# Sample readouts packed on TensorE's row and column groups, and head norms with tokens on partitions, in a hybrid decoder step

## The chip, the core and the metric

The kernel runs on one core of a Trainium2 chip. The metric is the device time of one execution in microseconds (us), and less is better. TensorE is called PE in the profile, its weight loads PEld, VectorE DVE, ScalarE ACT, GpSimd POOL and SyncE SP.

## The reference, cut to what matters

The program is one inference step of a two-layer trunk with model width 1024, for a prompt of 512 tokens and for 8 samples of one token each (520 columns, N). Layer 0 begins with a mixer of four GLA heads (key width 64, value width 128) and four retention heads (128 and 128); each head has a recurrent state matrix:

```python
    z = x @ w_in                      # q_g, k_g, v_g, a_lr, r_g, q_r, k_r, v_r, g_r
    # per head: S_t = diag(a_t) S_{t-1} + k_t^T v_t,  o_t = q_t S_t, in chunks over the prompt
    o_g, s_gla = chunked_gated_linear_attention(...)
    o_g = rms_head_norm(o_g, g_gla) * jax.nn.silu(heads(r_g, GLA_HEADS))
    o_r, s_ret = chunked_gated_linear_attention(...)
    o_r = group_norm_heads(o_r, g_ret, b_ret) * jax.nn.silu(heads(g_r, RET_HEADS))
    y = jnp.concatenate([o_g, o_r], axis=-1) @ w_out
```

The prompt starts from a zero state. Each of the 8 samples has a state of its own for each head: it is decayed, the outer product of the sample's key and value is added, it is stored, and it is read with the sample's query. The head norms are over the 128 values of one head at one token. What follows (layer norm, a gated ConvFFN, a short-convolution mixer, another ConvFFN) is not changed.

## The kernel before

Activations stand with features on partitions and the 520 tokens along the free axis. A weight unit is 1024 rows by 256 columns; SP loads it into one of three buffers, ACT makes its rounded part `w_hi` (`stage_hi`, line 332) and DVE the rest `w_lo` (`stage_lo`, line 339). PE makes a tile of 128 output features from it with three products for each of eight pieces of the contraction, in two halves of 256 and 264 tokens: 48 matmuls in lines 350 to 352.

The input projection has 15 units. Tiles 24 in number, of units 3 to 14, are numbered n = 0 to 23, and the attention is threaded between them. On PE the lists `inside[n]` (between the halves of tile n) and `after[n]` say which piece of attention is issued where; ACT has two such lists of its own, and DVE has `steps`, where every odd step begins with a `stage_lo`. ACT takes tile n out of PSUM (`tile_out`, line 1055, with SiLU for the last eight tiles) and at even n makes `w_hi` of a unit. Everything on an engine runs in the order in which it is written; semaphores bind the engines. Attention works in PSUM banks 4 to 7.

- Levels 0 to 7 (line 562) make the GLA scores: 16 matmuls a level with a contraction of 64.
- `gla_outputs` (lines 600 and 602) makes the outputs of the prompt with the values stationary. Products of contraction 128 (scores) and 64 (states) alternate.
- Samples: `outer(i)` (lines 682 and 685) makes k^T v for 8 samples by one matmul of contraction 8 with a block-diagonal `v_blk` from POOL (line 984), for six groups of heads one after the other. DVE adds it to the state (lines 1527 and 1532). `sample_out(i)` (lines 695 and 698) reads each state of each sample with a matmul of its own whose stationary operand is the state and whose moving operand is one column.
- Head norms: squares on ACT (line 1158), their sums over partitions by PE with the squares stationary and one column of ones moving (`hn_sums`, line 707), the mean of the retention heads by a centering matrix (line 729), root, reciprocal, and the spreading of the inverse over partitions by PE (`hn_spread`, line 716), partly inside the output projection.
- `project_short(0, ...)` is the output projection; its first tile pair goes step by step (lines 369 and 373) behind `head_hi` (ACT) and `head_lo` (DVE).

A matmul on float32 operands shows as two records in the trace, one on float32r as one.

Of the kernel before, what the change touches and what calls it, by code (L numbers as in the profile page):

```python
# [37 lines left out]
P = 128  # L38
# [3 lines left out]
NS = 8  # L42
# [60 lines left out]
def build(nc, x_prompt, x_sample, state_gla, state_ret, state_conv, state_ffn, w_mix_in, w_gla_gate_up,  # L103
# [19 lines left out]
    with ctx:  # L123
# [23 lines left out]
        centering = place("centering", [P, P], F32)  # L147
# [3 lines left out]
        w_up = place("w_up", [RANK, 2 * P], F32, at[0])  # L151
        last_rows = place("last_rows", [P, NU, 2 + NS], F32)
# [13 lines left out]
        o_att = [v_g[:, h, :] for h in range(GH)] + [v_r[:, h, :] for h in range(RH)]  # L166
# [14 lines left out]
        sq = slot("sq", 40, [P, 4, N])  # L181
        tok_r = place("tok_r", [NS, 8, P], F32, H + 38 * B)
        v_blk2 = place("v_blk2", [NS, NS, DV], F32, H + 34 * B)
# [15 lines left out]
        tok_s = place("tok_s", [NS, 8, P], F32)  # L199
        v_blk = place("v_blk", [NS, NS, DV], F32)  # L200
# [3 lines left out]
        inv = place("inv", [P, KD, 5], F32)  # L204

# [188 lines left out]
        v_blocks = [v_blk, v_blk2]  # L394
# [91 lines left out]
        def _(e):  # L486
# [62 lines left out]
            def level(n):  # L549

                if n == 0:
                    e.wait_ge(sem("gate_read"), 1)
                    e.wait_ge(sem("q_scaled"), 1)
                else:
                    e.wait_ge(sem("level_made"), n)
                    e.wait_ge(sem("level_added"), n)
                for h in range(GH):
                    p = slice((h % 2) * GDK, (h % 2 + 1) * GDK)
                    for c in range(NC):
                        t = slice(c * C, (c + 1) * C)  # L560
                        k, q = (k_t, q_t) if n else (k_g, q_g)
                        mm = e.matmul(bank(4 + h, P, c * C, C), k[p, h // 2, t], q[p, h // 2, t], start=True, stop=True)  # L562
# [16 lines left out]

            def gla_increments(cs):  # L580

                e.wait_ge(sem("gk_copied"), 1)
                for c in cs:
# [7 lines left out]
            def gla_outputs():  # L591
# [3 lines left out]
                for h in range(GH):  # L595
                    p = slice((h % 2) * GDK, (h % 2 + 1) * GDK)
                    for c in range(NC):
                        t = slice(c * C, (c + 1) * C)
                        out = bank(4 + h, P, c * C, C)
                        mm = e.matmul(out, v_tok[:, c, h * DV:(h + 1) * DV], sc[:, h, t], start=True, stop=(c == 0))  # L600
                        if c:
                            mm = e.matmul(out, state_g[p, c - 1, h // 2, :], q_t[p, h // 2, t], start=False, stop=True)
                mm.then_inc(sem("gla_out"), 1)

            def ret_scores():
# [1227 lines left out]
```

## Time and profile before

| | us |
|---|---|
| median of 3 runs (lowest, highest) | 1383.95 (1382.09, 1386.24) |
| the profiled execution, its own time | 1383.89 |
| its span in the profile | 1382.1 |
| PE busy in the span | 1337.5 |
| DVE busy | 680.3 |
| ACT busy | 483.9 |
| POOL busy | 116.6 |

The span is the time from the first to the last instruction on record; the execution has 1.8 us more around it. Busy time of PE says little of how fast it works, since a matmul at half clock is busy too; so the granted clock is read beside it.

### The profile page before, as it was taken

Reading aid. Unit: us, or ns where it says so; the run is one execution under the profiler, and the core shown is the slowest. Engines: PE = TensorE matmul, PEld = TensorE weight load, DVE = VectorE, ACT = ScalarE, POOL = GpSimd, SP = SyncE. Lnnn points to the kernel's source line nnn. Section 1 sums busy time; section 2 is a strip of 40 time slices with the busy share of each in tenths; the row PEclk is TensorE's granted clock in tenths of the full one; section 3 lists DMA queues with packets and bytes.
Section 4 is the critical chain, followed back from the end, with each engine's and each line's share of the span. In section 5 each row is a group of like instructions: output and inputs, shape, how many; then the busy total and the mean of one; then the engine's idle time right before and its main releaser. Section 6 shows DMA issues by size and latency. Waiting matters only on the chain.

```text
span 1382.1 us, 23804 instructions
## 1 busy us (share of the span) xinstructions
PE 1337.5 (97%) x10767; PEld 1311.0 (95%) x10767; DVE 680.3 (49%) x958; ACT 483.9 (35%) x697; POOL 116.6 (8%) x108
## 2 busy tenths in 40 slices
PE   7999999999989999999999899999899999999995
PEld 6999999899979999999999899999799999999995
DVE  4546933135556555555224444444575656562225
ACT  3433232122364444443121543332653434351111
POOL 3000003100240000000000410001600000000003
PEclk9999998689999999999999999999999999999998
DMA  8132212411122222222321222221132222222321
GB/s 258 62 93 62 65 62 67 129 58 61 63 71 89 92 93 93 93 93 86 105 91 54 92 92 92 92 93 63 62 123 92 92 92 92 92 84 85 121 84 62
DMA packets 123593, 122.46 MB, mean 89 GB/s; under 512 B 2482, under 2 KB 121165, under 8 KB 123477
## 3 DMA queue, kind: packets, MB, share of 16 engines
q1 hardware_dynamic: 112916, 115.32, 25.9%
q10 hardware_dynamic: 10432, 5.24, 1.3%
q8 instruction: 84, 1.38, 0.4%
q0 software_dynamic: 144, 0.39, 0.1%
q14 instruction: 17, 0.13, 0.0%
HBM read 114.79 MB, written 6.55 MB: 88 GB/s over the span
## 4 chain that ended last, share of the span: by engine, by line
PE 92%; ACT 3%; POOL 2%; DVE 1%; DMA 1%; issue 0%; POOLq 0%; ACTq 0%; SPq 0%
PE ps L350 26%; PE ps L352 25%; PE ps L351 25%; PE ps L369 3%; PE ps L562 2%; PE ps L373 2%; POOL ln_s L1011 1%; ACT x_hi L1233 1%; ACT x L1234 1%; POOL x_lo L1015 1%; PE ps L695 1%; PE ps L707 1%; PE ps L698 1%; ACT w_hi L332 1%; PE ps L497 1%; PE ps L685 1%
## 5 line engine op out<-in xcount | busy, mean ns | idle before, releaser
L350 PE MATMUL ps<-x_hi,w_hi 128*128 128x256 f32 (+1 forms) x2048 | 590.5, 288 | 0.7 <-ACT a_samp L1049 0.7
L352 PE MATMUL ps<-x_hi,w_lo 128*128 128x256 f32 (+1 forms) x2048 | 584.8, 286 | 0.0
L351 PE MATMUL ps<-x_lo,w_hi 128*128 128x256 f32 (+1 forms) x2048 | 582.9, 285 | 0.0
L350 PEld LDWEIGHTS ps<-x_hi,w_hi 128*128 128x128 f32 x2048 | 392.8, 192 | 3.7 <-issue 1.9
L351 PEld LDWEIGHTS ps<-x_lo,w_hi 128*128 128x128 f32 x2048 | 393.7, 192 | 0.1
L352 PEld LDWEIGHTS ps<-x_hi,w_lo 128*128 128x128 f32 x2048 | 392.6, 192 | 0.0
L339 DVE TENSOR_TENSOR w_lo<-w_raw,w_hi 128x2048 fp32r<-128x2048 f32 (+2 forms) x103 | 235.6, 2288 | 154.3 <-ACT w_hi L332 153.9
L350 PE MATMUL ps<-h_hi,w_hi 128*128 128x264 f32 (+1 forms) x896 | 255.0, 285 | 0.6 <-DVE x L1606 0.5
L351 PE MATMUL ps<-h_lo,w_hi 128*128 128x264 f32 (+1 forms) x896 | 252.8, 282 | 0.0
L352 PE MATMUL ps<-h_hi,w_lo 128*128 128x264 f32 (+1 forms) x896 | 252.7, 282 | 0.0
L332 ACT ACTIVATE w_hi<-w_raw 128x2048 fp32r<-128x2048 f32 (+2 forms) x103 | 192.6, 1870 | 155.1 <-DMA w_raw<-in_w_ffn_out 140.8
L350 PEld LDWEIGHTS ps<-h_hi,w_hi 128*128 128x128 f32 x896 | 168.4, 188 | 1.2 <-DVE w_lo L339 0.7
L352 PEld LDWEIGHTS ps<-h_hi,w_lo 128*128 128x128 f32 x896 | 168.7, 188 | 0.0
L351 PEld LDWEIGHTS ps<-h_lo,w_hi 128*128 128x128 f32 x896 | 168.6, 188 | 0.1
L1295 ACT ACTIVATE tmp<-ps,vecs 128x520 f32<-128x520 f32 x88 | 68.8, 784 | 203.6 <-PE ps L352 199.6
L1759 DVE TENSOR_TENSOR tmp<-tmp,past_ffn 128x8 f32<-128x8 f32 x88 | 15.0, 171 | 134.8 <-ACT last_rows L1296 134.7
L1606 DVE SCALAR_TENSOR_TENSOR x<-x,ps 128x256 f32<-128x256 f32 (+1 forms) x64 | 26.7, 422 | 99.2 <-PE ps L352 99.1
L1763 DVE SCALAR_TENSOR_TENSOR tmp<-ps,vecs,tmp 128x510 f32<-128x510 f32 x88 | 65.9, 748 | 3.1
L1760 DVE SCALAR_TENSOR_TENSOR tmp<-ps,vecs,tmp 128x511 f32<-128x511 f32 x88 | 65.4, 744 | 0.0
L373 PE MATMUL ps<-x_lo,w_hi 128*128 128x256 f32 (+1 forms) x192 | 56.7, 295 | 9.0 <-POOL x_lo L1015 8.9
L369 PE MATMUL ps<-x_hi,w_hi 128*128 128x256 f32 (+1 forms) x192 | 57.0, 297 | 3.8 <-DVE w_lo L339 2.8
L1011 POOL TENSOR_TENSOR ln_s<-tmp 128x256 f32<-128x256 f32 (+1 forms) x6 | 8.6, 1425 | 607.1 <-ACT tmp L1217 607.1
(240 smaller groups left out, 1231.3 us busy)
## 6 DMA issues: line engine op xcount, KB each, us to landing
w_raw<-in_w_ffn_in SPq DMA_DIRECT2D x44, 1024.0 KB, 4.9
w_raw<-in_w_ffn_out SPq DMA_DIRECT2D x16, 1024.0 KB, 5.1
w_raw<-in_w_mix_in SPq DMA_DIRECT2D x14, 1024.0 KB, 5.1
w_raw<-in_w_sc_in SPq DMA_DIRECT2D x12, 1024.0 KB, 5.0
w_raw<-in_w_ffn_out SPq DMA_DIRECT2D x8, 768.0 KB, 4.4
w_raw<-in_w_mix_out SPq DMA_DIRECT2D x4, 1024.0 KB, 5.1
w_raw<-in_w_sc_out SPq DMA_DIRECT2D x4, 1024.0 KB, 5.0
x_tok<-in_x_prompt SPq DMA_DIRECT2D x2, 1024.0 KB, 7.4
```

Source lines behind the costliest of these rows:

```text
L332: e.activation(w_hi[:, u % WB, 0:k, 0:c], w_raw[:, u % WB, 0:k, 0:c], ACT.Copy).then_inc(hi_made, 1)
L339: e.tensor_tensor(w_lo[:, u % WB, 0:k, 0:c], w_raw[:, u % WB, 0:k, 0:c], w_hi[:, u % WB, 0:k, 0:c].bitcast(F32), ALU.subtract).then_inc(lo ...
L350: e.matmul(out, wh, xh[:, k, lo:hi], start=(first and i == 0), stop=False)
L351: e.matmul(out, wh, xl[:, k, lo:hi], start=False, stop=False)
L352: mm = e.matmul(out, wl, xh[:, k, lo:hi], start=False, stop=(last and i == len(ks) - 1))
L369: e.matmul(out(half), w, xh[:, k, lo:hi], start=(k == 0 and w is wh), stop=False)
L373: mm = e.matmul(out(half), wh, xl[:, k, lo:hi], start=False, stop=(k == KD - 1))
L562: mm = e.matmul(bank(4 + h, P, c * C, C), k[p, h // 2, t], q[p, h // 2, t], start=True, stop=True)
L1295: e.activation(tmp[:, slot, :], acc(slot), ACT.Identity, bias=ffn_vec(l, 3, tile), scale=ffn_vec(l, 2, tile))
L1606: e.scalar_tensor_tensor(x32[:, t, lo:hi], x32[:, t, lo:hi], ALPHA, out_acc(q, h), ALU.mult, ALU.add).then_inc(out_free, 1)
L1760: e.scalar_tensor_tensor(t[:, 1:T], acc(slot)[:, 0:T - 1], ffn_vec(l, 1, tile), t[:, 1:T], ALU.mult, ALU.add).then_inc(sem("tap_done"), 1)
L1763: e.scalar_tensor_tensor(t[:, 2:T], acc(slot)[:, 0:T - 2], ffn_vec(l, 0, tile), t[:, 2:T], ALU.mult, ALU.add).then_inc(tile_free, 1)
```

## The change

For the samples, keys, values and queries of four heads are copied by POOL into columns 32h of a tile `pack`, and two transposes put the keys and values of head h and its 8 samples on partitions 32h to 32h+7. One masked multiply makes `v_blk` for four heads. The outer products of the heads are then issued side by side, each with its own 32 rows of the array. The readout has the queries stationary (32 columns a head) and the states moving (512 columns); it gives every query against every state, DVE keeps the pairs that belong together by a mask and sums eight blocks. The outputs of the prompt are made with tokens on partitions (scores, or queries, stationary); `gla_outputs` issues all products of contraction 128 first and then those of 64. Head statistics are made by `bn_stats` and `bn_aggr` on DVE (17 groups of a kind); the GLA outputs are scaled on DVE, the retention outputs by 17 activations on ACT (`hn_norm`). PE then transposes the eight heads back (`heads_turn`), two at a time after tiles 20 to 23. Level 1 computes 64 by 64 of each block, all that is used of it. Two more state buffers (`samp2`) let retention states load earlier.

```diff
-        o_att = [v_g[:, h, :] for h in range(GH)] + [v_r[:, h, :] for h in range(RH)]
+        o_tok = [slot("o_tok_g", 8, [P, NC, 512]), slot("o_tok_r", 12, [P, NC, 512])]
+        o_fin = slot("o_fin", 22, [P, 8, N])
...
+                        if n == 1:
+                            s, t = slice(c * C, c * C + C // 2), slice(c * C + C // 2, (c + 1) * C)
+                            out = bank(4 + h, C // 2, c * C + C // 2, C // 2)
...
+            def samples_turn(kind):
+
+                e.wait_ge(sem("packed"), kind + 1)
+                if kind:
+                    e.wait_ge(sem("rk_decayed"), 1)
+                for i in range(2):
+                    tr = e.transpose(bank(6, P, i * P, P), pack[:, 3 * kind + i, :], ident[:, :])
+                tr.then_inc(sem("samp_turned"), 1)
...
+                for c in range(NC):
+                    for h in range(GH):
+                        e.matmul(bank(4 + h, P, c * DV, DV), sc[:, h, c * C:(c + 1) * C], v_tok[:, c, h * DV:(h + 1) * DV],
+                                 start=(c == 0), stop=(c == 0), skip_group_check=True)
+                for c in range(1, NC):
+                    for h in range(GH):
+                        p = slice((h % 2) * GDK, (h % 2 + 1) * GDK)
+                        mm = e.matmul(bank(4 + h, P, c * DV, DV), q_t[p, h // 2, c * C:(c + 1) * C], state_g[p, c - 1, h // 2, :],
+                                      start=False, stop=True, skip_group_check=True)
...
+            def gla_outer():
+
+                e.wait_ge(sem("gla_copied"), 1)
+                e.wait_ge(sem("v_blk_made"), 1)
+                for half in range(2):
+                    for h in range(GH):
+                        r, d, b = 32 * h, (h % 2) * GDK, 4 + 2 * (h // 2) + half
+                        mm = e.matmul(ps_t[d:d + GDK, b * 512:(b + 1) * 512], tok_s[r:r + NS, 0, d:d + GDK],
+                                      v_blk[r:r + NS, 4 * half:4 * half + 4, :], start=True, stop=True)
+                mm.then_inc(sem("outer_summed"), 1)
+
+            def gla_samples_out():
+
+                e.wait_ge(sem("rs_decayed"), 1)
+                for half in range(2):
+                    for h in range(GH):
+                        r, d = 32 * h, (h % 2) * GDK
+                        mm = e.matmul(ps_t[r:r + 32, (4 + half) * 512:(5 + half) * 512], pack[d:d + GDK, Q_G, r:r + 32],
+                                      samp[d:d + GDK, h // 2, 4 * half:4 * half + 4, :], start=True, stop=True)
+                mm.then_inc(sem("samp_read"), 1)
...
             def ret_keys():
-                e.wait_ge(sem("rs_decayed"), 1)
+                e.wait_ge(sem("samp_masked"), 1)
...
+            def ret_outer(hs):
+
+                e.wait_ge(sem("v_blk_made"), 2)
+                if hs[0]:
+                    e.wait_ge(sem("samp_made"), 4)
...
+                for half in range(2):
+                    for h in hs:
+                        r = 32 * h
+                        mm = e.matmul(bank(4 + 2 * (h % 2) + half), tok_s[r:r + NS, 2, :], v_blk[r:r + NS, 4 * half:4 * half + 4, :],
+                                      start=True, stop=True)
+                mm.then_inc(sem("outer_summed"), 1)
+
+            def ret_samples_out():
+
+                e.wait_ge(sem("samp_made"), 2 + RH)
+                for half in range(2):
+                    for h in range(RH):
+                        r = 32 * h
+                        mm = e.matmul(ps_t[r:r + 32, (4 + half) * 512:(5 + half) * 512], pack[:, Q_R, r:r + 32],
+                                      samp_of[h][:, 4 * half:4 * half + 4, :], start=True, stop=True)
+                mm.then_inc(sem("samp_read"), 1)
...
+            def heads_turn(hs):
+
+                kind = hs[0] // GH
+                e.wait_ge(sem("hn_normed"), (1, 18)[kind])
+                if hs[0] == 0:
+                    e.wait_ge(sem("samp_masked"), 2)
+                elif hs[0] == 6:
+                    e.wait_ge(sem("head_read_r"), 2)
+                else:
+                    e.wait_ge(sem("head_read_g"), hs[0])
                 for h in hs:
+                    o, j = (2 + h % 2) * 1024 + 256, h % GH
+                    for c in range(NC):
+                        e.transpose(ps_t[:, o + c * C:o + (c + 1) * C], o_tok[kind][:, c, j * DV:(j + 1) * DV], ident[:, :])
+                    r = slice(32 * j, 32 * j + NS)
+                    tr = e.transpose(ps_t[:, o + T:o + N], o_samp[r, kind, :], ident[r, r])
+                    tr.then_inc(sem("head_turned"), 1)
...
-                [gla_values], [gla_keys], [lambda: gla_increments((0, 1))], [lambda: gla_increments((2, 3))],
-                [gla_outputs], [ret_scores], [ret_keys], [gla_samples_turn], [lambda: ret_chunks((0, 1))],
-                [ret_samples_turn], [lambda: outer(1), lambda: sample_out(0)], [lambda: outer(3), lambda: sample_out(2)],
-                [lambda: outer(5), lambda: sample_out(4)], [lambda: hn_sums(0)], [lambda: hn_spread(2), lambda: hn_spread(3)],
-                [lambda: hn_center((GH + 2, GH + 3))]]
-            inside = [[] for _ in range(16)] + [
-                [ret_values], [lambda: ret_chunks((2, 3))], [lambda: outer(0)],
-                [lambda: outer(2), lambda: sample_out(1)], [lambda: outer(4), lambda: sample_out(3)],
-                [lambda: sample_out(5)], [lambda: hn_spread(0), lambda: hn_spread(1)], [lambda: hn_center((GH, GH + 1))]]
+                [gla_values], [gla_keys, lambda: samples_turn(0)], [lambda: gla_increments((0, 1))], [lambda: gla_increments((2, 3))],
+                [gla_outputs], [gla_outer], [ret_scores], [ret_keys], [ret_values], [lambda: ret_chunks((2, 3))],
+                [lambda: ret_outer((0, 1))], [lambda: ret_outer((2, 3))], [lambda: heads_turn((0, 1))], [lambda: heads_turn((2, 3))],
+                [lambda: heads_turn((4, 5))], [lambda: heads_turn((6, 7))]]
+            inside = [[] for _ in range(15)] + [
+                [gla_samples_out], [lambda: samples_turn(1)], [lambda: ret_chunks((0, 1))], [], [], [ret_samples_out], [], [], []]
...
+            def hn_norm():
+
+                e.wait_ge(sem("hn_shifted"), 1)
+                for i in range(17):
+                    x = o_tok[1][:, i // RH, (i % RH) * DV:(i % RH + 1) * DV] if i < 16 else o_samp[:, 1, :]
+                    e.activation(x, x, ACT.Identity, bias=hn_shift[:, i:i + 1], scale=hn_inv[:, 1, i:i + 1]).then_inc(sem("hn_normed"), 1)
...
+                     [gla_decays, gla_values], [gla_keys, lambda: samples_copy(0)], [], [], [gla_outputs], [], [gla_samples_store], [],
+                     [ret_values], [lambda: ret_outputs((2, 3)), lambda: ret_samples_load((2, 3))],
+                     [], [lambda: ret_samples_store((0, 1))], [lambda: ret_samples_store((2, 3))],
+                     [lambda: hn_root(1), lambda: head_hi((0, 1))], [hn_norm, lambda: head_hi((2, 3))], [lambda: head_out((4, 5))]]
             inside = [[] for _ in range(16)] + [
+                [lambda: samples_copy(1), lambda: hn_root(0)], [lambda: ret_samples_load((0, 1)), lambda: ret_outputs((0, 1))],
+                [], [], [], [], [], []]
...
+                [lambda: rotate(k_r, (2, 3), 7)], [ret_queries, gla_sample_states], [ret_scores, lambda: head_parts(0, range(NC))],
+                [lambda: samples_masked(0), lambda: samples_summed(0), lambda: head_stats(0), ret_keys], [],
+                [lambda: ret_states((0, 1)), lambda: head_inverse(0)], [lambda: ret_states((2, 3)), lambda: head_parts(1, range(NC))],
+                [lambda: ret_sample_states((0, 1))], [lambda: ret_sample_states((2, 3)), lambda: samples_masked(1), lambda: samples_summed(1),
+                lambda: head_stats(1)], [lambda: head_gated((0, 1)), lambda: head_inverse(1)], [lambda: head_gated((2, 3)), lambda: head_lo((0, 1))],
+                [lambda: head_lo((2, 3))]]
```

## Rows read from the trace of the kernel before

**Rows 1.** The page: PE's granted clock in 40 slices of 34.6 us, in tenths.
```profile
PEclk9999998689999999999999999999999999999998
```
**Rows 2.** Windows: stretch, its length, busy by engine, PEclk, DMA share, GB/s.
```profile
163.07:173.86 10.79, 10.79 (x58) 7.89 (x56) 10.23 (x13) 2.40 (x2) 1.09 (x2) 1.00 0.03 12
...
224.08:286.31 62.23, 62.23 (x306) 53.59 (x305) 15.12 (x22) 8.65 (x16) 11.54 (x7) 0.67 0.37 107
286.31:321.81 35.50, 34.71 (x258) 33.89 (x258) 13.27 (x18) 12.63 (x18) 0.00 (x0) 0.90 0.18 60
321.81:341.62 19.81, 18.19 (x137) 17.74 (x138) 11.46 (x16) 4.73 (x7) 0.00 (x0) 0.91 0.00 1
```
**Rows 3.** Groups of PE, 163 to 342 us: busy, mean ns of one, idle before.
```profile
L695 PE MATMUL ps<-q_g,samp 64*128 64x1 f32 x64 | 11.1, 330 | 0.0
L707 PE MATMUL ps<-ones,sq 128*128 128x1 f32 x80 | 10.8, 270 | 0.8 <-DVE v_r L1540 0.8
L698 PE MATMUL ps<-q_r,samp 128*128 128x1 f32 x64 | 10.0, 286 | 0.0
L716 PE MATMUL ps<-ident,inv 128*128 128x128 f32 (+1 forms) x80 | 9.2, 266 | 0.0
L685 PE MATMUL ps<-v_blk,tok_r 8*128 8x512 f32 x16 | 8.2, 632 | 0.0
...
L682 PE MATMUL ps<-v_blk,tok_s 8*64 8x512 f32 x16 | 4.2, 600 | 0.0
L729 PE MATMUL ps<-v_r,centering 128*128 128x256 f32 (+1 forms) x16 | 3.8, 382 | 0.0
```
**Rows 4.** Windows of one half tile each (24 matmuls of lines 350 to 352).
```profile
217.26:220.26 3.00, 3.00 (x27) 2.98 (x26) 0.00 (x0) 0.60 (x1) 2.38 (x2) 1.00 0.21 87
226.27:230.89 4.62, 4.62 (x26) 4.48 (x25) 2.16 (x8) 0.00 (x0) 3.56 (x2) 0.63 0.00 0
...
250.75:256.33 5.58, 5.58 (x25) 5.34 (x24) 0.00 (x0) 2.46 (x6) 0.00 (x0) 0.50 0.33 94
```
**Rows 5.** Timeline of PE at `gla_outputs` and `ret_chunks`: start, duration.
```profile
163.61 0.48 PE L602 MATMUL ps<-q_t,state_g 64*128 64x128 f32 x2
164.03 0.49 PE L600 MATMUL ps<-sc,v_tok 128*128 128x128 f32 x2
...
204.66 1.05 PE L646 MATMUL ps<-v_tok,k_tok 128*128 128x128 f32 x8
205.55 1.06 PE L655 MATMUL ps<-sc,v_tok 128*128 128x128 f32 x8
```
**Rows 6.** The chain that ended last, in order of time: start, us, what.
```profile
73.28 2.75 PE ps L562 x32
...
230.96 1.87 PE ps L682 x8
...
243.79 1.91 PE ps L685 x4
```
**Rows 7.** Groups of DVE by form, whole span.
```profile
L339 DVE TENSOR_TENSOR w_lo<-w_raw,w_hi 128x2048 fp32r<-128x2048 f32 x94 | 219.4, 2335 | 136.1 <-ACT w_hi L332 135.7
...
L1495 DVE TENSOR_TENSOR sc<-ps,decay 128x512 f32<-128x512 f32 x4 | 2.5, 682 | 7.0 <-PE ps L611 7.0
...
L1703 DVE BATCH_NORM_STATS2 y_stats<-ps 128x6 f32<-128x256 f32 x16 | 5.6, 417 | 8.0 <-PE ps L809 4.3 <-PE ps L811 3.7
...
L1710 DVE BATCH_NORM_AGGREGATE y_mean<-y_stats 128x2 f32<-128x24 f32 x4 | 0.8, 234 | 0.1
```
**Rows 8.** Groups of ACT by form, whole span.
```profile
L332 ACT ACTIVATE w_hi<-w_raw 128x2048 fp32r<-128x2048 f32 x94 | 179.7, 1911 | 120.4 <-DMA w_raw<-in_w_ffn_out 106.1 <-DMA w_raw<-in_w_mix_out 7.5 <-DMA w_raw<-in_w_sc_in 4.9
...
L1055 ACT ACT_TABLE_LOAD x2 | 2.6, 1283 | 0.9 <-PE ps L352 0.9
```
**Rows 9.** Timeline of ACT in a layer norm: start, duration.
```profile
374.93 0.59 ACT L1234 ACTIVATE x<-x,vecs 128x256 f32<-128x256 f32 x1
375.42 0.59 ACT L1233 ACTIVATE x_hi<-x,vecs 128x256 fp32r<-128x256 f32 x1
```

More of the change, by code:

```diff
@@ L594, in gla_outputs @@
                 e.wait_ge(sem("gla_state"), NC)
[L595 to L602, printed above, removed]
@@ L704, in token_sums @@
-            def token_sums(out, squares, start=True, stop=True):
-                for j in range(5):
-                    t0 = j * P if j < 4 else N - P
-                    mm = e.matmul(out[:, j:j + 1], squares[:, t0:t0 + P], ones[:, 0:1], start=(start and j == 0), stop=stop,
-                                  skip_group_check=True)
-                return mm
-            def spread(slot_, inv_):
-                for j in range(5):
-                    n = P if j < 4 else NS
-                    o = slot_ * 1024 + 256 + j * P
-                    mm = e.matmul(ps_t[:, o:o + n], inv_[:, j:j + 1].broadcast_to([P, P]), ident[:, P - n:P],
-                                  start=True, stop=True)
-                return mm
@@ L1160, in hn_root @@
-            def hn_root(grp):
-                e.wait_ge(sem("hn_var"), grp + 1)
-                e.activation(inv[:, 4 * grp:4 * grp + 4, :],
-                             bank(4, P, 32 * grp, 32).rearrange("p (h j) -> p h j", h=4)[:, :, 0:5],
-                             ACT.Sqrt, bias=eps[:, :], scale=1.0 / DV).then_inc(sem("hn_root"), 1)
+                    if h < 2:
+                        e.wait_ge(sem("samp_read"), 1)
+                        e.wait_ge(sem("samp_stored%d" % h), 32)
+                    else:
+                        e.wait_ge(sem("ret_out"), NC)
@@ new lines, in hn_norm, with head_out @@
+            def hn_norm():
[3 more added lines that the diff above has]
+                    e.activation(x, x, ACT.Identity, bias=hn_shift[:, i:i + 1], scale=hn_inv[:, 1, i:i + 1]).then_inc(sem("hn_normed"), 1)
+            def head_out(hs):
+                for h in hs:
+                    e.wait_ge(sem("head_turned"), h + 1)
+                    e.activation(o_fin[:, h, :], acc(2 + h % 2), ACT.Identity, bias=vec(V_LN, COL_BR + h - GH),
+                                 scale=vec(V_LN, COL_GR + h - GH)).then_inc(sem("head_read_r"), 1)
@@ L1199, in _ @@
                     piece()
-            hn_root(1)
-            head_hi(range(GH, KD))
+            head_hi((4, 5))
+            head_out((6, 7))
+            head_hi((6, 7))
             def rows_back(n, tiles):
@@ L1361, in _ @@
             stage_lo(e, 2)
+            for h in range(4):
+                e.tensor_copy(samp_mask[32 * h:32 * (h + 1), :], ident[32 * h:32 * (h + 1), 32 * h:32 * h + NS])
             e.wait_ge(sem("past_turned"), 1)
@@ L1534, in sample_states @@
[L1534 to L1546 removed]
+                    ins.then_inc(sem("samp_made"), 1)
```

329 lines of the change are left out of this document (152 added, 177 removed).

## The prediction

> **What bounds the kernel now.** I began with the page's clock line: PE runs at full clock except in slices 7 to 9, some 240 to 345 us into the span [rows 1]. Then windows of that region: PE is busy for 62.2 of 62.2 us and 34.7 of 35.5, so it hardly waits; but it is granted 0.67 and 0.90 of its clock, and 0.91 in the start of the output projection [rows 2]. The groups of PE say what it does there beside the projection's tiles: 128 small float32 records with one moving column each for the sample readouts, 80 more for sums of squares, 80 that spread inverses, and outer products over 512 columns with a contraction of 8 [rows 3]. So the attention stage is bound by PE's own sequence, and any work taken off PE there comes off the time, as long as DVE and ACT keep up. Windows of single half tiles show the second cost: the same 24 matmuls take 3.00 us at full clock, 4.62 where 0.63 is granted and 5.58 at 0.50 [rows 4]. 1.00 and 0.50 are the two levels, 2.4 and 1.2 GHz. PE did not idle before it fell; it ran the small products of the samples.
>
> I compare the stretch from the start of `gla_outputs` (163.1 us) to the end of the projection's first tile pair (341.6), 178.5 us. Behind it nothing changes. The sum is made against the profiled execution, 1383.9 us, which is the median of the runs (1383.95).
>
> **What PE no longer does.** Outer products and readouts: 11.1 + 10.0 + 8.2 + 4.2 = 33.5 us busy [rows 3]; the tail of each of twelve stretches overlaps what follows by 0.1 or so, so 32.4. Norm sums, spreads and centering: 10.8 + 9.2 + 3.8 and a wait of 0.8, less overlaps, 23.3 [rows 3]. `gla_outputs` now takes 10.8 for 56 records [rows 2], because products of contraction 128 and of 64 alternate: two records cost 0.42, where eight of contraction 128 in a row cost 0.89, 0.11 each [rows 5]. In the new order there is one switch: 32 x 0.11 + 24 x 0.086 (a level's 32 records of contraction 64 take 2.75 [rows 6]) + 0.4 = 6.0, a gain of 4.8. Between strictly alternating row groups the 24 could also cost 0.21 each, which would leave 2. Transposes for samples and level 1 at a quarter of its area: about 1.5 less (bounds 0.5 and 2.5).
>
> Half clock: seven half tiles, the first and the third shown in [rows 4], take 34.3 us for 20.7; 13.6 could come back. In the first tile pair of the projection 16 steps of 0.72 (six matmuls of 0.12, from [rows 4]) are 11.6; it takes 19.8 [rows 2], of which the spreads are counted above (4.2), 1.6 is half clock and 2.4 waits for `h_lo` and for a `w_lo` that DVE makes too late. After the change the norms end earlier against the staging, so the 2.4 goes. Removed in all: 32.4 + 23.3 + 4.8 + 1.5 + 13.6 + 1.6 + 2.4 = 79.6 us.
>
> **What PE gets.** Five packed pieces. A 512-column record of 128 output columns takes 1.91 / 4 = 0.48; with 64 output columns 8 records take 1.87, 0.23 each [rows 6]: half the columns, two in flight. For 32 columns I carry this on to 0.12, so 16 records of each readout cost 1.9. `gla_outer` (64 columns, four row groups) lies between 3.7 (columns alone) and 1.9; I take 2.8. `ret_outer` (128 columns, two row groups) lies between 3.8 and 1.9, twice; 2.4 each, since the levels' 0.086 a record against 0.11 says that row groups overlap at least at their borders [rows 5, 6]. Sum 11.4; from 9.5 to 30.6, if nothing overlaps (48 x 0.48 + 2 x 3.8).
>
> The Trainium skill, "TensorE: Matmul & The Clock Gate", Part 3, measured a speedup of 3.07 for four row tiles of 512 columns and 2.38 for three column tiles. By 3.07 the estimate for a readout is 2.5 rather than 1.9, and the five pieces would come to some 2 us more. No row here shows four in flight.
>
> `heads_turn`: per head eight records of 0.11 and two with a contraction of 8, which switch the array's tiling: 0.42 and some 0.1 more by [rows 5]; 1.4 a head, 11.2 for eight (7 to 12). Sum of both 22.6.
>
> **Where PE will wait.** I walk the three lists. ACT stages a unit in 1.9 [rows 8], DVE in 2.3; four DVE operations over 512 columns take 2.5; `bn_stats` over 256 columns takes 0.42, so for 128 columns, back to back, I put 0.22; `bn_aggr` 0.15 to 0.2 [rows 7].
> - `ret_keys` (after tile 15) waits for `samp_masked`. DVE runs scores 2.5, 16 `bn_stats` 3.5, `stage_lo` 2.3, mask 1.2 against 4.9 of PE's readout and half tile, and the wait is 1.9.
> - `samples_turn(1)`, inside tile 16, waits for `rk_decayed`, behind sums, 17 `bn_aggr` and `ret_keys`: 1.4 + 3.3 + 2.5, against PE's 1.7 + 2.9; wait 2.6.
> - `ret_chunks((0,1))`, inside tile 17, waits for values that ACT now copies after `hn_root(0)`, an activation table load of 1.3 [rows 8], `tile_out` and `stage_hi`: 1.3.
> - `heads_turn((4,5))`, after tile 22, waits for all 17 activations of `hn_norm`. ACT has these behind `tile_out(22)` (0.6) and `stage_hi` (1.9). One activation with scale and bias over 256 columns starts 0.49 after the last one [rows 9]; for 128 columns I put 0.37, 6.3 in all. PE stands for 8.7 us (6.6 to 12). Tile 23, and behind it the whole projection, is queued there.
> - `heads_turn((6,7))`, after tile 23, waits for `head_out((4,5))`: on ACT `tile_out`, a table load and two activations, 3.6.
>
> Sum 18.1 (11 to 24). The transfers don't set it: SP's units wait for the same tiles as before, three units ahead, and retention states load earlier. Stores leave ACT's queue some 10 us and more before `norm(0)` waits for them. POOL's masks and copies are ready 10 us before PE wants them.
>
> **The clock after.** What went before the falls in the old kernel, contractions of 8 for 2 us, is still there three times. I put 3 us for them, and 2.5 for tile 23 after the long wait (a half tile at 0.50 costs 2.6 more [rows 4]). 5.5, bounds 0 and 13.
>
> **Sum.** 22.6 + 18.1 + 5.5 = 46.2 against 79.6: 33 us less. 1383.9 - 33 = 1351 us.
>
> By another page of the Trainium skill, "TensorEngine Tiling (Array Packing)", Gotcha 1, different row tiles cannot write the same PSUM bank at one time. `gla_samples_out` does just that: heads 0 and 1 have different 64-row groups and one bank. By it that piece would take 3.8 and the sum would be 1353. No row of before has this case.
>
> **Rivals.**
> - *No overlap in the packed pieces* (a tiling that runs one record at a time): 19 us more, of which the early DVE waits swallow a part; 1366 to 1370. For it: the single-file 0.48 of [rows 6] is the only rate seen with 128 columns. Against it: 0.23 for 64. Chance 0.12.
> - *The waits dissolve and the clock stays up*: `hn_norm` at 0.25 an activation, tile 23 hardly slowed, no fall after the packed pieces; 12 us less than my sum, 1339. For it: four heads side by side make each piece short. Chance 0.17.
> - *Slower*: the clock stays at 0.50 from `gla_outer` to the end of `hn_norm`. Everything that PE does there at full speed, some 100 us, would cost up to 100 more. It decides from 33 us on: if PE spends 66 us or more at half clock beyond what I have. Against it: even with one-column products for 60 us the mean was 0.67, and one undisturbed tile brought it back [rows 2, 4]. At its likeliest 1395. Chance 0.03.
> - *The change gives nothing*, because DVE's longer list (statistics, masks, sums, scaling, some 25 us more) makes PE wait wherever it saves: about 1383. DVE is busy only 15.1 of 62.2 us in the worst stretch [rows 2], so there is room. Chance 0.03.
> - *My sum*, 1351, chance 0.65; its own range is 1343 to 1361.
>
> Two such kernels can be told apart from about 0.3% (4 us). The range from 1338 to 1366 leaves out the end of the no-overlap case, both unfavourable ones, and the lower edge. Faster 0.94, within 0.3% 0.02, slower 0.04.
>
> **What the next profile would show.** PE's records in a readout: 16 within 2 us (right) or 7 us (no overlap). `gla_outputs` near 6 us. PEclk near 1.0 in slices 7 to 9, with dips right behind outer products and behind one long wait. In the list of waits PE behind ACT's `hn_norm` for 6 to 12 us, the longest of all; behind DVE's mask and `ret_keys` 2 to 3 each. The first tile pair of the projection in under 12.5 us, ending near 309. The prediction falls if `heads_turn` costs much above 1.4 a head, if `bn_aggr` is far from 0.2, or if PE's wait moves to a place that the walk holds free, `ret_samples_out` or `ret_outer((2,3))`, where it leaves less than 1 us.

## The result, and the profile after

| | before | after |
|---|---|---|
| median, us (lowest, highest; 4 runs each) | 1383.02 (1379.24, 1386.24) | 1341.59 (1341.03, 1341.77) |
| span of the profiled execution, us | 1382.1 | 1339.2 |

The ratio is 0.9698, 95% interval 0.9681 to 0.9715: 41 us less, where 33 less were forecast. 1341.6 lies inside the stated range of 1338 to 1366, nine below the sum's 1351, and just outside the sum's own range, which began at 1343.

The page of the kernel after: the heading, busy time by engine, and the granted clock in 40 slices of 33.5 us.
```profile
span 1339.2 us, 23409 instructions
...
PE 1278.6 (95%) x10525; PEld 1254.3 (94%) x10525; DVE 690.4 (52%) x1033; ACT 487.9 (36%) x703; POOL 107.7 (8%) x109
...
PEclk9999999979999999999999999999999999999998
```
One dip is left, in slice 9, where [rows 1] had three slices under full clock. Windows of the kernel after say where (stretch, length, PE busy, PEclk, DMA share, GB/s): `gla_outputs`, the four kinds of packed piece in the order of the program, the two stretches with a fallen clock, and the first tile pair of the output projection.
```profile
162.09:167.37 5.28, 5.28 (x57) 1.00 0.06 25
...
173.32:175.20 1.88, 1.88 (x18) 1.00 0.31 53
187.55:189.40 1.85, 1.85 (x18) 1.00 0.03 9
227.58:229.50 1.92, 1.92 (x10) 1.00 0.02 4
240.39:242.25 1.86, 1.86 (x18) 1.00 1.04 323
...
265.50:275.90 10.40, 6.87 (x33) 0.53 0.00 0
282.50:289.00 6.50, 6.14 (x27) 0.50 0.15 52
285.30:298.40 13.10, 13.10 (x96) 0.86 0.00 1
```
`gla_outputs` took 10.79 before [rows 2]. The pair ended at 341.62 [rows 2] and ends at 298.40. So the stretch on which the forecast was made, 178.5 us long, is 136.3 (162.09 to 298.40), and it starts 1.0 us earlier: 43.2 in all, against 42.9 between the spans. The whole gain lies there.

PE's groups, 130 to 290 us: count, busy, mean ns of one, idle time before and what ended it.
```profile
L733 PE MATMUL ps<-ident,o_tok_r 128*128 128x128 f32 x16 | 4.4, 432 | 12.7 <-ACT o_samp L1160 9.0 <-ACT o_fin L1166 3.7
...
L733 PE MATMUL ps<-ident,o_tok_g 128*128 128x128 f32 x16 | 2.5, 279 | 0.0
L735 PE MATMUL ps<-ident,o_samp 8*128 8x8 f32 x8 | 2.0, 248 | 0.0
...
L633 PE MATMUL ps<-v_blk,tok_s 8*64 8x512 f32 x16 | 1.9, 600 | 0.0
L716 PE MATMUL ps<-samp,pack 128*32 128x512 f32 x16 | 1.9, 599 | 0.0
L643 PE MATMUL ps<-samp,pack 64*32 64x512 f32 x16 | 1.9, 595 | 0.0
```
These stand where [rows 3] had 57 us of small products. A record of L716 lasts 599 ns and sixteen of them 1.86 us: some five at a time, by the records' own lengths, which are modelled. Their starts say four: in `gla_outer` and both readouts four records start within 0.02 us of each other, the next four 0.45 to 0.48 us later, and each further four 0.43 us after the last. And the list of PE's waits, whole span up to 460 us:
```profile
PE ps L733 <- ACT o_samp L1160: 9.0, 1, 9.0
PE ps L733 <- ACT o_fin L1166: 3.7, 1, 3.7
...
PE ps L596 <- DVE k_tok L1509: 1.2, 1, 1.2
PE ps L660 <- DVE samp_prod_g L1554: 1.2, 1, 1.2
PE ps L679 <- ACT v_tok L1117: 1.2, 1, 1.2
PE ps L617 <- DVE state_g L1474: 0.9, 1, 0.9
```
L733 is `heads_turn`, L596 `samples_turn(1)`, L660 `ret_keys`, L679 `ret_chunks((0,1))`, L617 `gla_outputs`. The longest wait is for `hn_norm`. ACT's timeline there (start, duration, what; idle before it in brackets):
```profile
260.04 0.60 ACT L1053 ACTIVATE g_r<-ps 128x520 f32<-128x520 f32 x1 [2.70 <-PE ps L356]
260.54 1.90 ACT L336 ACTIVATE w_hi<-w_raw 128x2048 fp32r<-128x2048 f32 x1
262.34 6.25 ACT L1160 ACTIVATE o_tok_r<-o_tok_r,hn_shift,hn_inv 128x128 f32<-128x128 f32 x16
268.50 0.48 ACT L1160 ACTIVATE o_samp<-o_samp,hn_shift,hn_inv 128x128 f32<-128x128 f32 x1
```
PE stands from the end of tile 22 (260.0) to 269.0. ACT works all that time, but it stood idle for 2.70 us just before, waiting for PE's tile.

### The profile page after: what moved, and what is told of

It is laid out like the page before. It is cut to its first block, busy times and chain, and to the rows that moved or that the text cites. A ratio compares the mean times of both kernels' runs of the same rounds, so it can differ in the third digit from the quotient of the medians.

```text
span 1339.2 us, 23409 instructions
## 1 busy us (share of the span) xinstructions
PE 1278.6 (95%) x10525; PEld 1254.3 (94%) x10525; DVE 690.4 (52%) x1033; ACT 487.9 (36%) x703; POOL 107.7 (8%) x109
## 4 chain that ended last, share of the span: by engine, by line
PE 87%; ACT 4%; DVE 3%; POOL 3%; issue 1%; DMA 1%; POOLq 0%; ACTq 0%; SPq 0%
PE ps L354 25%; PE ps L356 25%; PE ps L355 25%; PE ps L373 3%; POOL ln_s L1009 2%; PE ps L377 2%; PE ps L572 2%; ACT x_hi L1239 1%; ACT x L1240 1%; POOL x_lo L1013 1%; ACT w_hi L336 1%; PE ps L502 1%; PE ps L733 0%; ACT o_tok_r L1160 0%; DMA x_tok<-in_x_sample 0%
## 5 line engine op out<-in xcount | busy, mean ns | idle before, releaser
L354 PE MATMUL ps<-x_hi,w_hi 128*128 128x256 f32 (+1 forms) x2048 | 584.6, 285 | 0.7 <-ACT a_samp L1047 0.7
L354 PEld LDWEIGHTS ps<-x_hi,w_hi 128*128 128x128 f32 x2048 | 387.0, 189 | 6.7 <-issue 5.1
L355 PEld LDWEIGHTS ps<-x_lo,w_hi 128*128 128x128 f32 x2048 | 388.1, 190 | 0.1
L356 PEld LDWEIGHTS ps<-x_hi,w_lo 128*128 128x128 f32 x2048 | 387.2, 189 | 0.0
L373 PE MATMUL ps<-x_hi,w_hi 128*128 128x256 f32 (+1 forms) x192 | 56.3, 293 | 3.1 <-DVE w_lo L343 2.8
```

The costliest lines, as they stand in the source:

```text
L354: e.matmul(out, wh, xh[:, k, lo:hi], start=(first and i == 0), stop=False)
L355: e.matmul(out, wh, xl[:, k, lo:hi], start=False, stop=False)
L356: mm = e.matmul(out, wl, xh[:, k, lo:hi], start=False, stop=(last and i == len(ks) - 1))
L373: e.matmul(out(half), w, xh[:, k, lo:hi], start=(k == 0 and w is wh), stop=False)
```

## The experiments

Ten kernels ran. Times are medians with the lowest and highest run; a ratio is to the kernel before, run beside it on the same chip. "The gain" of an edit to the kernel after is worked out against 1341.59.

**norm_first.** `hn_norm` ahead of `tile_out(22)` and the staging:
```diff
-                     [lambda: hn_root(1), lambda: head_hi((0, 1))], [hn_norm, lambda: head_hi((2, 3))], [lambda: head_out((4, 5))]]
+                     [lambda: hn_root(1), hn_norm, lambda: head_hi((0, 1))], [lambda: head_hi((2, 3))], [lambda: head_out((4, 5))]]
```


> The changed kernel, with hn_norm put on ACT's list before tile_out(22) and stage_hi instead of behind them. Theory (the 9.0 us for which PE stands before heads_turn((4,5)) is on the path that sets the end, and so is the half clock behind it): the activations then end about 6.5 us earlier, PE waits 2 to 3 us there, tile 23 runs at or near full clock, and the time falls by 7 to 11 us from 1341.6, to 1331 to 1335. Rival (the wait only stands in for another one, since w_hi and tile_out of tile 22 come 6 us later): the time stays within 2 us of 1341.6.

1334.85 (1330.11 to 1335.95), ratio 0.9656 (0.9614 to 0.9699). PE's waits from 225 to 290 us:
```profile
PE ps L733 <- ACT o_fin L1166: 3.7, 1, 3.7
PE ps L733 <- ACT o_samp L1160: 2.2, 1, 2.2
```
and windows of the two stretches with a fallen clock:
```profile
263.90:270.70 6.80, 6.80 (x33) 0.51 0.00 0
277.70:284.90 7.20, 7.20 (x35) 0.55 0.08 26
```
The long wait went from 9.0 to 2.2 us and the kernel gained 6.7, which is that wait and no more. The time is as expected, but the expectation had tile 23 at or near full clock, and its first half ran at half clock: PE's clock still fell behind the wait that was left, and behind the other one. One of the four runs took 1330.11, with a mean clock of 0.994 against 0.988 and 0.989 in the others; no trace of it says where.

**norm_n20.** `hn_root(1)` and `hn_norm` one tile earlier still, behind tile 20, where ACT was idle; `head_out((4,5))` one tile earlier; DVE makes the inverse before it scales heads 0 and 1.
```diff
-                     [], [lambda: ret_samples_store((0, 1))], [lambda: ret_samples_store((2, 3))],
-                     [lambda: hn_root(1), lambda: head_hi((0, 1))], [hn_norm, lambda: head_hi((2, 3))], [lambda: head_out((4, 5))]]
+                     [], [lambda: ret_samples_store((0, 1))], [lambda: ret_samples_store((2, 3)), lambda: hn_root(1), hn_norm],
+                     [lambda: head_hi((0, 1))], [lambda: head_hi((2, 3)), lambda: head_out((4, 5))], []]
...
-                lambda: head_stats(1)], [lambda: head_gated((0, 1)), lambda: head_inverse(1)], [lambda: head_gated((2, 3)), lambda: head_lo((0, 1))],
+                lambda: head_stats(1)], [lambda: head_inverse(1), lambda: head_gated((0, 1))], [lambda: head_gated((2, 3)), lambda: head_lo((0, 1))],
```


> The changed kernel with hn_root(1) and hn_norm behind tile 20 on ACT, head_inverse(1) before head_gated((0,1)) on DVE, and head_out((4,5)) behind tile 22. Theory (both waits of PE at the end, 9.0 and 3.7 us, and two spells of 1.2 GHz of some 10 and 6 us that follow them are the price of an order on ACT): no wait over 1 us in the head part, PEclk 1.00 from tile 21 to the projection, 16 to 19 us less than 1341.6, so 1323 to 1326. Rival (the clock falls for the 8-column transposes or the readouts and not for the waits): the waits go, the spells stay, and it gains 12 to 13 us only, 1329.

1324.26 (1323.78 to 1325.07), ratio 0.9587 (0.9548 to 0.9625). Both waits are gone, and the clock is at full up to the projection and in its first pair:
```profile
245.00:255.00 10.00, 10.00 (x81) 1.00 0.48 149
255.00:268.13 13.13, 13.13 (x107) 1.00 0.15 49
268.13:281.00 12.87, 12.87 (x108) 1.00 0.24 82
```
The gain is 17.3 us, where the two waits together were 12.7. The work that ran at half clock behind them adds to it: by the trace of the kernel after, 2.4 us in the four later turns, 1.8 in tile 23 and 1.5 in the projection's first pair, 5.7 in all. Together that is 18.4, and by the starts of PE's records the stretch from `gla_outputs` to the end of the first pair is 18.3 shorter. Some 1.5 us are lost again in the layer norm behind the projection, where the clock fell behind a wait of 2.2 us in this kernel and not in the kernel after: the same work takes 9.0 us (329.54 to 338.57) for 7.5 (348.32 to 355.80). The packed outer products and the transposes are all still there, and no clock falls behind them. So the waits, and not the small products, brought it down in the kernel after.

**alternate.** `gla_outputs` with contractions of 128 and 64 in turn again, all else as after:
```diff
-                for c in range(1, NC):
-                    for h in range(GH):
+                        if c == 0:
+                            continue
```


> The changed kernel with the products of contraction 128 and 64 of gla_outputs alternating again. Theory (a switch between 128 and 64 rows costs about 0.1 us a record and side, whichever operand is stationary): the 56 records take about 10.8 us instead of 5.3, and the time rises by 5 to 6 us to 1347. Rival (the gain came from the swap of stationary and moving operands, or from starting on other banks): under 7 us for the 56 records, within 2 us of 1341.6.

1347.28 (1346.80 to 1347.61), ratio 0.9752 (0.9705 to 0.9799).
```profile
162.02:172.88 10.86, 10.86 (x56) 1.00 0.03 12
```
The same 56 records take 10.86 us for 5.28, and all of it, 5.7 us, arrives at the end. **b_grouped** is the counterpart, the order changed in the kernel before alone (all products of contraction 128, then those of 64; values still stationary):

> The kernel before, with only the order in gla_outputs changed: all products of contraction 128 first, then those of 64; the values stay stationary. Theory (the switches alone cost 5.5 of its 10.8 us): 5.3 us for the 56 records, and 1383 falls by 5 to 6 us to about 1378. Rival (the swap of operands is needed for it, or PE then waits for a state that it got later before): within 2 us of 1383.

1378.04 (1374.06 to 1380.90, 10 runs) against 1381.57 (1374.78 to 1387.05, 14 runs); ratio 0.9972 (0.9953 to 0.9990). Its groups in `gla_outputs`:
```profile
L598 PE MATMUL ps<-sc,v_tok 128*128 128x128 f32 x31 | 3.6, 275 | 0.0
L604 PE MATMUL ps<-q_t,state_g 64*128 64x128 f32 x24 | 1.6, 280 | 0.0
```
The piece shrinks by 5.6 us here too, but some 3.5 arrive; the interval of the ratio allows 1.4 to 6.5, so it is not shown that less arrives than the piece lost. Later in this kernel the stretches at half clock lie elsewhere than in the kernel before, and which of the small products they fall on changes with any shift; the kernel before itself spreads over 12 us from run to run, the kernel after over less than one. A part of a clock-bound stretch is a poor place to measure a few microseconds.

**head_major.** The two loops of each packed piece swapped, so that neighbouring records are at the same place of the array:
```diff
-                for half in range(2):
-                    for h in range(GH):
+                for h in range(GH):
+                    for half in range(2):
```
(so in `gla_outer`, `gla_samples_out`, `ret_outer` and `ret_samples_out`)

> The changed kernel with the loops over heads and halves swapped in the five packed pieces, so that the two halves of one head, which use the same place of the array, come one after the other. Theory (matmuls start in their written order and only neighbours at different places of the array overlap): the readouts take 4 to 7 us each instead of 1.9, the outer products 3 to 4, together 10 to 20 us more on PE and a time of 1350 to 1360, with half clock possible. Rival (PE lets work overlap whatever the order, or the low rate comes from the narrow stationary operand alone): each piece stays near 1.9 us and the time within 2 us of 1341.6.

1341.85 (1340.93 to 1343.19), ratio 0.9714 (0.9675 to 0.9754): no change. In its chain the pieces start and last as follows:
```profile
173.52 1.90 PE ps L633 x16
227.78 1.92 PE ps L706 x8
235.64 1.92 PE ps L706 x8
240.60 1.87 PE ps L716 x16
```
The idea that neighbours must be at different places fell. What fits every piece is this: a piece costs what its busiest place has to do, four records of some 0.47 us, in whatever order they are issued. In this kernel too the records of `gla_outer` and of the readouts start four by four, the groups 0.43 us apart.

**one_place.** The test of that: every record uses the whole array, as many records and moving columns as before. The samples' outputs are no longer the reference's.
```diff
-                        mm = e.matmul(ps_t[d:d + GDK, b * 512:(b + 1) * 512], tok_s[r:r + NS, 0, d:d + GDK],
-                                      v_blk[r:r + NS, 4 * half:4 * half + 4, :], start=True, stop=True)
+                        mm = e.matmul(bank(b), tok_s[:, 0, :],
+                                      v_blk[:, 4 * half:4 * half + 4, :], start=True, stop=True)
...
-                        mm = e.matmul(ps_t[r:r + 32, (4 + half) * 512:(5 + half) * 512], pack[:, Q_R, r:r + 32],
+                        mm = e.matmul(bank(4 + half), pack[:, Q_R, :],
```
(likewise in `gla_samples_out` and `ret_outer`)

> The kernel after, but each outer product and each readout of the samples uses the whole of TensorE's array in place of one of its places: the outer products of both layers take all 128 rows of their tile (and v_blk's), the readouts a stationary of 128 columns for 32. The number of instructions, their 512 moving columns and all of the work around them stay; the outputs of the samples are no longer the reference's. The theory is that the five kinds of packed piece take 1.85 to 1.92 us for 16 records (1.9 for 8 in each of the two ret_outer) because records at different places run side by side, and a piece costs what the busiest place has, 4 records of about 0.47. If so, records that all use the same rows come one after the other: 16 x 0.47 = 7.5 us for gla_outer and for each of the two readouts, 8 x 0.47 = 3.8 for each ret_outer, 30.1 us in all where 9.4 stood. Of these 20.7 us some hides in the waits of 1.2 us for VectorE before ret_keys and samples_turn(1), so some 17 to 21 us are left and the kernel takes 1358 to 1362. The rival is that the low time for a record comes from elsewhere (the short stationary, or 128 columns for outputs that lie in few banks); then the pieces stay near 1.9 us and the kernel stays at 1341 to 1343.

1355.27 (1355.14 to 1355.92), ratio 0.9784 (0.9763 to 0.9805). The chain:
```profile
173.47 6.87 PE ps L633 x16
192.49 6.88 PE ps L643 x16
234.55 3.43 PE ps L706 x8
243.73 3.43 PE ps L706 x8
250.00 6.87 PE ps L716 x16
```
0.43 us a record, 27.5 in all for 9.4: packing is worth 18.1 us of PE here. Of these 13.7 arrive, less than the 17 to 21 that were expected (1358 to 1362). The starts of PE's records say where the rest is: what follows the pieces is delayed by 17.1 us, since the ends of the pieces overlap with their neighbours, and the two waits for VectorE that are gone from PE's list (1.2 us each there) take back 2.8, for VectorE gets the time that PE loses. Behind the last piece the delay is 14.3, and the two stretches at half clock change it by less than 0.5. The theory had the mechanism and, at 0.47 a record, a price too high by a tenth: 0.47 is the mean of four with the ends of the piece, and the step from one record to the next at the same place is 0.43 in both kernels.

This edit changes the width of the stationary operand together with the place, and so does not answer by itself whether a narrow one (32 columns in the readouts, 64 in `gla_outer`) makes a record short. The starts in the kernel after do: the groups follow each other by 0.43 us at 32, 64 and 128 columns alike, as the full-width records do here, so the gain is in the number side by side.

**b_noread, b_noouter, b_neither.** Three edits of the kernel before that ask which of its small products cost what. The first keeps one of each eight one-column products in `sample_out`; the second lets `outer` move 32 columns for 512; the third does both. Each leaves out that part of the samples' results.
```diff
-                        for s in range(NS):
+                        for s in range(1):
...
-                        rhs = v_blocks[h % 2][:, 4 * half:4 * half + 4, :]
+                        rhs = v_blocks[h % 2][:, 4 * half:4 * half + 4, 0:8]
```


> The kernel before, with one instead of eight one-column matmuls per readout; the readouts of samples 1 to 7 are left out, the outer products and states stay. PE loses 7/8 of 20.4 us, 17.8 us. Theory (the one-column matmuls are what brings the clock down): the seven slow half tiles come back to 3.0 us but for those behind the norm sums, 12 us more, together about 30 less, 1353. Rival (the outer products of contraction 8 bring it down): the fall stays, 18 to 22 us less, 1361 to 1365.

> The kernel before, with outer products of 32 instead of 512 columns (15/16 of each is left out), readouts unchanged. PE loses about 15/16 of 12 us, at least 8 us, since a record has a least duration. Theory (one-column matmuls bring the clock down): half clock stays in most of 230 to 290 us; 8 to 12 us less, 1371 to 1375. Rival (outer products bring it down): PEclk near 1.0 there, 20 us less or more, 1363 or below.

> The kernel before with both edits that were made to it singly: the outer products move 32 columns for 512, and one of each eight readout products of one column is kept. The samples' outputs are no longer the reference's. Alone the second gained 19.4 us (1362.15 against 1381.57) and the first 14.7 (1366.87), and with either the granted clock still fell several times between 230 and 307 us. The theory is that both kinds of small work bring the clock down, so that together they give back more than the sum of the two, 34 us: the clock stays at 1.00 up to the sums of the head norms, and the kernel takes 1336 to 1345. The rival is that the clock falls for another reason (the sums of the norms, or the waits), that the two gains only add up or overlap, and that the kernel takes 1347 to 1355 with half-clock stretches where they were.

| kernel | median (lowest, highest) | ratio (interval) |
|---|---|---|
| b_noread | 1362.15 (1360.56, 1365.23) | 0.9862 (0.9825, 0.9899) |
| b_noouter | 1366.87 (1366.34, 1368.95) | 0.9898 (0.9866, 0.9929) |
| b_neither | 1358.46 (1356.94, 1359.41) | 0.9805 (0.9786, 0.9824) |

Windows from 217 to 330 us of, in this order, the kernel before, b_noread, b_noouter and b_neither:
```profile
217.00:330.00 113.00, 112.21 (x678) 0.77 0.29 87
```
```profile
217.00:330.00 113.00, 109.16 (x737) 0.89 0.32 96
```
```profile
217.00:330.00 113.00, 110.46 (x806) 0.86 0.31 96
```
```profile
217.00:330.00 113.00, 104.03 (x765) 0.89 0.31 96
```
Either edit alone gives back two fifths to a half of the clock that was missing, so neither kind of product was the one cause, and neither single theory held: b_noread came out where its rival had it, with 19.4 us less, and b_noouter, with 14.7 less, between its theory and its rival. Together they gain 26 us, less than the two single gains (34) and far from a full recovery: the theory for b_neither fell. Its waits and its windows tell why. PE's waits in the same stretch, and DVE's:
```profile
PE ps L698 <- DVE samp L1532: 6.2, 3, 4.1
...
DVE samp L1532 <- DMA samp<-in_state_ret: 17.9, 4, 7.0
```
Windows of the half tile behind the wait of 4.1 us; of `hn_sums` (40 products of one column, twice) and of the half tile behind each:
```profile
244.78:251.54 6.76, 6.76 (x30) 0.52 0.57 155
...
260.88:266.16 5.28, 5.28 (x42) 0.82 0.59 202
266.16:271.42 5.26, 5.26 (x25) 0.50 0.00 0
289.17:295.00 5.83, 5.83 (x40) 0.76 0.32 115
295.00:300.17 5.17, 5.17 (x29) 0.61 0.00 0
```
With PE's sample work gone, the loading of the retention states through two buffers becomes the pace: DVE waits 17.9 us for those transfers, where it waited 7.9 in the kernel before, and PE waits for DVE. And the sums of the head norms bring the clock down by themselves: both half tiles behind them run at half clock, wholly or in the main (0.50 and 0.61). Waits of 1.5 and 0.8 us stand shortly before the two here, but in the kernel before the first of them has none: PE runs without a gap at 1.00 from 285 us, makes the sums from 289.3 to 293.7, and is at 0.50 from 294.3. In the kernel after, with four buffers, DVE's list of waits from 150 to 300 us has no transfer at all. So the samples' products were not all that held the kernel before back: behind them stood the loads and the sums on PE, and the change removes those too. How much of the gain the two more buffers are worth by themselves stays open; the kernel after with two was not tried.

**no_waits.** norm_n20 with three more orders, meant for the three waits of 1.2 us:
```diff
-                     [ret_values], [lambda: ret_outputs((2, 3)), lambda: ret_samples_load((2, 3))],
+                     [], [lambda: ret_outputs((2, 3)), lambda: ret_samples_load((2, 3))],
...
+                if n == 16:
+                    ret_values()
...
-                [lambda: rotate(k_r, (2, 3), 7)], [ret_queries, gla_sample_states], [ret_scores, lambda: head_parts(0, range(NC))],
-                [lambda: samples_masked(0), lambda: samples_summed(0), lambda: head_stats(0), ret_keys], [],
+                [lambda: rotate(k_r, (2, 3), 7)], [ret_queries, gla_sample_states], [ret_scores],
+                [lambda: samples_masked(0), lambda: head_parts(0, range(NC)), ret_keys, lambda: samples_summed(0), lambda: head_stats(0)], [],
...
-                if n % 2 == 1:
+                if n % 2 == 1 and n != 17:
...
+                if n == 17:
+                    stage_lo(e, 13)
```


> The kernel with hn_norm moved ahead (the one that took 1324.26 us), and three orders more: VectorE turns k_tok (ret_keys) before samples_summed(0) and head_stats(0), ScalarE runs ret_values before its part of tile 16's staging, and VectorE stages tile 13's lower half behind the states of ret. These are the works whose lateness TensorE waits for in three places of 1.2 us each: before samples_turn(1) for k_tok, before ret_chunks for v_tok, and before ret_keys for samp_prod_g. The theory is that TensorE's own instructions set the end from the tiles to the projection, so that each wait that goes shortens the kernel by itself: 2.4 us (two waits) to 3.6 (all three), 1320.7 to 1322. The rival is that VectorE is as late one step further on, so that the waits only move to the next instruction that needs it, and the time stays at 1323.5 to 1325.

1318.97 (1318.42 to 1319.82), ratio 0.9521 (0.9504 to 0.9539), and the page:
```profile
PEclk9999999999999999999999999999999999999998
```
Its list of PE's waits from 0 to 460 us has none of the three, and between the layer's start-up and the projection only this one is left:
```profile
PE ps L617 <- DVE state_g L1476: 0.9, 1, 0.9
```
The rival, that the waits only move, is out. The spans differ by 5.1 us (1322.1 and 1317.0). From the start of `gla_outputs` to the start of the projection the traces give 106.4 and 102.2 us, 4.3 less, of which 3.6 are the waits; the rest of the span gained another 0.8, which is 0.9 lost at the start of the program and 1.7 gained behind the start of the projection, most of it (1.5) in a layer norm near 720 us, where half clock fell at different places in the two traces. At 1319 us it is 4.8% faster than the kernel before and 1.7% faster than the kernel after.

## Why the prediction was right, and where its sum was off

The direction, the stretch, the two longest waits and their order were as forecast, and the price of packing within 2 us. The sum itself was 9 us off, and nearly all of what PE gets came out below its term. The time came out next to the rival of 1339, but not by its mechanism: that rival had `hn_norm` at 0.25 an activation and tile 23 hardly slowed, and the long wait came in full with half clock behind it. The terms, against the trace of the kernel after:

| term | forecast | measured |
|---|---|---|
| five packed pieces | 11.4 | 9.4 (1.88 + 1.85 + 2 x 1.92 + 1.86) |
| `heads_turn` | 11.2 | 7.8, of which 2.4 is half clock |
| `gla_outputs`, now | 6.0 | 5.3 |
| the five waits | 18.1 | 16.3 (1.2 + 1.2 + 1.2 + 9.0 + 3.7) |
| a wait not forecast, before `gla_outputs` | 0 | 0.9 |
| clock, outside the turns | 5.5 | 3.3 (tile 23 1.8, first pair 1.5) |
| sum | 52.2 | 43.0 |

That is 9.2 us less than forecast, and with the 33.4 of the sum (79.6 - 46.2) it makes 42.6, against 42.9 between the spans. So what PE no longer does was right in total; its terms were not measured one by one. One of them was read wrongly: of the 2.4 us of waits in the old first pair the trace shows 1.6 (1.1 for `h_lo`, 0.5 for DVE at the pair's end), and none there for `w_lo`.

- **`heads_turn` was the mis-sized step**, "per head eight records of 0.11 and two with a contraction of 8". A transpose is one record, not the two of a float32 matmul: L733 has 16 records for four heads of four chunks, and L735 one a head. At full clock a head takes 0.7 us (0.53 to 0.59 and 0.16), half of the 1.4. Against that, the four later heads ran at half clock, which I had not charged to them: 1.25 each.
- **Packed pieces: right in kind, 2 us too dear.** I took 2.8 for `gla_outer` and 2.4 for each `ret_outer`, between full overlap and none. They take 1.88 and 1.92, the lower bound. one_place, head_major and the starts of the records show the rule behind it. The rival "no overlap" is out: it would look like one_place.
- **Gotcha 1 did not bite.** `gla_samples_out`, with heads of different row groups writing one bank, takes 1.85 us, as long as `ret_samples_out`, whose heads share all their rows. By an estimate from the Trainium skill, "TensorEngine Tiling (Array Packing)", Gotcha 1, it would have taken 3.8; the measurement decides against that reading of the rule. The speedup of 3.07 for four row tiles in the Trainium skill, "TensorE: Matmul & The Clock Gate", Part 3, is below what these float32 records give, 6.87 / 1.88 = 3.7. From that speedup the prediction made the five pieces "some 2 us more"; by its own terms it is 0.9 (0.6 more for each readout, 0.3 less for `gla_outer`).
- **The waits were found by walking the lists, and the two large ones to 0.3 us**: 9.0 for 8.7 and 3.7 for 3.6. An activation of 128 columns with scale and bias costs 0.38 (6.15 us for 16) where I had put 0.37. The smaller ones came out at 1.2 for 1.9, 2.6 and 1.3: `bn_aggr` over 128 partitions takes 0.07 (17 in 1.24 us), not 0.15 to 0.2, and `bn_stats` 0.20 for 0.22. "`bn_aggr` is far from 0.2" was one of the signs by which the prediction was to fall; it came, and its effect stayed small, since it only shortened a wait.
- **The clock: right sum by luck, wrong place.** Half clock cost 5.7 us in all (2.4 in the turns, 3.3 outside them) where I had 5.5. I charged 3 us behind the outer products, since "contractions of 8 for 2 us" went before the falls in the old kernel. No fall came there; both came behind the waits of 9.0 and 3.7 us, and norm_n20, which has the same products and no such wait, keeps 1.00. Behind 9.0 I had 2.5 us, and the second wait I had left without a price.
- **What half clock cost the kernel before** was put at 13.6 us on seven half tiles. The kernel after shows none of these falls; its own two are those in the table. The b_ kernels show that this was no property of the readouts alone: outer products, readouts and norm sums each held it down.
- **A moved time**: I put the end of the first pair near 309; it is 298.4, by the same 9 us and the earlier start of the stretch.

## What to carry to other kernels

Where PE sets the end, price its small work by place: records on different rows or columns of the array run side by side in any order, and a piece costs what its busiest place has. Group products of one contraction; a change between 128 and 64 rows at every product doubled the cost of a piece. Then look for what PE now waits for, for a wait costs itself and the slow clock behind it: moving seventeen activations into a gap of ScalarE, with the small orders around it, gave 17 us, two fifths of what the whole change had given.

## What the runs showed of the hardware

- Four groups of rows or columns give 3.7 times the rate of one (6.87 against 1.88 and 1.85 us for 16 records of 512 columns), two groups 1.8 times (3.43 against 1.92 for 8), and the order of issue within a piece makes no difference. Records at one place follow each other by 0.43 us, with 32, 64 or 128 columns stationary.
- Alternating contractions of 128 and 64: 56 records in 10.86 us; grouped: 5.28. A float32 product is two records, so the first order changes the contraction 23 times and the second once: 5.6 us over 22 changes, 0.25 us each.
- The granted clock fell behind waits of PE of 1.5 (b_neither, 256.4 us), 2.2, 3.7, 4.1 and 9.0 us, and not behind those of 1.2 and 1.4; behind the wait of 2.2 us in the layer norm (L776) it fell in norm_n20 and in no_waits (0.58 and 0.68 in windows of 3 us) and stayed at 1.00 in the kernel after, so 2.2 us decides nothing by itself. And in the kernel before it fell with no wait behind 40 products of one column (`hn_sums`), but not behind sixteen packed products of 512 columns with a contraction of 8, nor behind the transposes of `heads_turn` in norm_n20.
